# Orders in the second mixer and at the start of the second feed-forward: means joined inside a column, picks ahead of low halves, a root and a Silu table earlier

## What is computed

```python
def hybrid_mixer(h, ...):                       # h = rms_norm(x, norm_mix_w)
    proj = h @ w_in                             # 512 pool, 256 q, 256 k, 512 v, 16 gate, 512 r
    pool_out = multiscale_pool(p, pool_w, pool_scale)
    log_g = log_sigmoid(g_low @ gk_w2 + gk_b) / 16
    o = gla_chunked(q, k, v, log_g)             # chunks of 64, causal inside and between
    gla_out = rms_norm(o, gla_norm_w) * silu(r)
    return concatenate([pool_out, gla_out]) @ w_out

def conv_ffn_2(h, w_up, conv_w, conv_b, w_down):
    u = h @ w_up                                # 2 x 2816 columns
    u = conv_b + conv_w[0]*u[t-2] + conv_w[1]*u[t-1] + conv_w[2]*u[t]
    return (silu(gate) * val) @ w_down
```

## Time and profile before

| | us |
|---|---|
| median of 3 runs | 849.12 (848.76 to 849.17) |
| the profiled execution's own time | 849.34 |
| its span in the trace | 847.3 |
| PE busy | 835.3 (99%) |
| DVE busy | 577.3 (68%) |
| ACT busy | 476.9 (56%) |
| POOL busy | 353.2 (42%) |

### The profile page before, as it was taken

How to read it: one execution, slowest core, us unless ns; L and a number is a source line. 1 busy time by engine, 2 the same in 40 slices (tenths; PEclk the granted TensorE clock), 3 DMA queues, 4 the chain that set the end, 5 groups by cost and what they waited for, 6 DMA issues and landing times.

```text
span 847.3 us, 14837 instructions
## 1 busy us (share of the span) xinstructions
PE 835.3 (99%) x5858; PEld 766.1 (90%) x5858; DVE 577.3 (68%) x1214; ACT 476.9 (56%) x793; POOL 353.2 (42%) x173
## 2 busy tenths in 40 slices
PE   9999999999999999999999999999999999999997
PEld 4578999998899999999999988999999888888886
DVE  4789879886467896767677879686448445444445
ACT  7353345443766655555555864555447666666665
POOL 0000000001751598888887300200000788888883
PEclk9999999999999999999999999999999999999999
DMA  9998556654275556555555546364535556566651
GB/s 350 367 384 272 202 208 214 206 168 140 73 253 182 175 182 194 178 193 176 184 189 176 162 150 197 101 194 127 179 100 174 174 177 198 183 195 191 198 178 73
DMA packets 44742, 161.37 MB, mean 190 GB/s; under 512 B 5105, under 2 KB 5377, under 8 KB 43522
## 3 DMA queue, kind: packets, MB, share of 16 engines
q1 hardware_dynamic: 44384, 159.38, 58.0%
q10 hardware_dynamic: 290, 1.05, 0.3%
HBM read 159.37 MB, written 1.05 MB: 189 GB/s over the span
## 4 chain that ended last, share of the span: by engine, by line
PE 87%; DVE 6%; ACT 3%; DMA 2%; issue 1%; POOL 1%; ACTq 0%; DVEq 0%; POOLq 0%
PE bank L667 13%; PE bank L672 13%; PE bank L670 12%; PE bank L1104 9%; PE bank L1110 5%; PE bank L1193 2%; PE bank L1195 2%; PE bank L1197 2%; PE bank L1143 2%; PE bank L1141 2%; PE bank L1145 2%; DVE wlo L526 2%; PE bank L1003 2%; PE bank L769 1%; PE bank L771 1%; PE bank L775 1%
## 5 line engine op out<-in xcount | busy, mean ns | idle before, releaser
L526 POOL TENSOR_TENSOR wlo<-raw,whi 128x1024 fp32r<-128x1024 f32 (+1 forms) x147 | 334.8, 2300 | 407.2 <-ACT whi L1375 407.0
L1375 ACT ACTIVATE whi<-raw 128x1024 fp32r<-128x1024 f32 (+1 forms) x253 | 258.6, 1026 | 66.7 <-PE bank L672 22.6
L1824 DVE SCALAR_TENSOR_TENSOR accs<-bank,vec,accs 128x189 f32<-128x189 f32 (+4 forms) x440 | 161.1, 433 | 71.2 <-ACT accs L1687 71.2
L526 DVE TENSOR_TENSOR wlo<-raw,whi 128x1024 fp32r<-128x1024 f32 x106 | 129.0, 1229 | 29.1 <-ACT whi L1375 28.4
L667 PE MATMUL bank<-h,whi 128*128 128x256 f32 x504 | 143.7, 286 | 0.0
L672 PE MATMUL bank<-h,whi 128*128 128x256 f32 x504 | 142.3, 283 | 0.0
L670 PE MATMUL bank<-h,wlo 128*128 128x256 f32 x496 | 140.5, 283 | 0.7 <-DVE wlo L526 0.7
L667 PEld LDWEIGHTS bank<-h,whi 128*128 128x128 f32 x504 | 96.6, 192 | 0.7 <-issue 0.3
L672 PEld LDWEIGHTS bank<-h,whi 128*128 128x128 f32 x504 | 96.7, 192 | 0.0
L670 PEld LDWEIGHTS bank<-h,wlo 128*128 128x128 f32 x496 | 95.1, 192 | 1.1 <-DVE wlo L526 1.0
L1104 PE MATMUL bank<-h,whi 128*128 128x512 f32 x352 | 88.4, 392 | 0.5 <-DVE gl L1821 0.4
(11 more groups left out here) (362 smaller groups left out, 1851.0 us busy)
## 6 DMA issues: line engine op xcount, KB each, us to landing
raw<-in_up SPq DMA_DIRECT2D x88, 512.0 KB, 3.5
raw<-in_w_in SPq DMA_DIRECT2D x45, 512.0 KB, 4.5
raw<-in_down SPq DMA_DIRECT2D x44, 512.0 KB, 3.5
ada_sc<-in_ada SPq DMA_DIRECT2D x8, 1024.0 KB, 19.9
ada_kT<-in_adaT SPq DMA_DIRECT2D x16, 512.0 KB, 4.7
raw<-in_w_out SPq DMA_DIRECT2D x16, 512.0 KB, 4.5
raw<-in_w_in_t SPq DMA_DIRECT2D x12, 512.0 KB, 4.5
ada_sc<-in_adaT SPq DMA_DIRECT2D x8, 512.0 KB, 7.7
```

The lines of the kernel that those rows point to most:

```text
L526: return e.tensor_tensor(wlo[:, j % HL, 0:k], raw[:, j % RAW, 0:k], whi[:, j % HL, 0:k].bitcast(F32), ALU.subtract)
L1375: e.activation(whi[:, j % HL, 0:(k1 - k0) * 128], raw[:, j % RAW, 0:(k1 - k0) * 128], ACT.Copy).then_inc(S.hi.up(j))
L1824: return e.scalar_tensor_tensor(out=out, in0=a, scalar=s, in1=b, op0=o1, op1=o2)
```

## The change

It moves instructions; it adds one activation (of one element a partition) that loads Silu's table. Nothing of the arithmetic changes.

1. `means("down")` moves from before column 7 to inside it, after its ninth matmul; column 0 moves ahead of the gate's small matmul, and `spread("rsd")` moves from inside column 7 to inside column 0. On ACT the high half of column 3's chunk (`splits(ch("w_in2", 0) + HL)`) moves ahead of Exp and Ln. On DVE column 0's low half moves from ahead of the mean's copy to behind the two reciprocals.
2. Columns 12 and 13 become `late`. On DVE the four picks of the first half of the tokens come ahead of the low halves of chunks 14 and 15 and ahead of column 12's scaling.
3. In the second feed-forward the root for `wo` comes ahead of one `splits`, and `spread("wo")` one k-tile later; Silu's table is loaded in pair 1 ahead of its second `splits`.

```diff
@@ lin_wide @@
-                    if beside and k == 2:
+                    if beside and k == 3:
@@ pe, second mixer @@
-            means("down", M["ssum"][:, 0, :], 4, S.sums, ("down", 7), (S.by_row, "rsd"))
             slot, free = lin_ring.take(("w_in2", 7), S.raw2, 7)
-            lin("w_in2", 7, banks[slot][:, 0:L], hm, free, lambda: spread("rsd", aux_bank("down")[:, L:2 * L]))
+            lin("w_in2", 7, banks[slot][:, 0:L], hm, free,
+                lambda: means("down", M["ssum"][:, 0, :], 4, S.sums, ("down", 7), (S.by_row, "rsd")))
+            slot, free = lin_ring.take(("w_in2", 0), S.raw2, 0)
+            lin("w_in2", 0, banks[slot][:, 0:L], hm, free, lambda: spread("rsd", aux_bank("down")[:, L:2 * L]))
             slot, free = lin_ring.take("gate_low", S.zb, "zb")
...
-            for n in range(4):
+            for n in range(1, 4):
...
             def readout(h):
                 slot, free = lin_ring.take(("w_in2", 12 + h), S.raw2, 12 + h)
-                lin("w_in2", 12 + h, banks[slot][:, 0:L], hm, free)
+                lin("w_in2", 12 + h, banks[slot][:, 0:L], hm, free, late=h < 2)
@@ act, feed-forward @@
+            def silu_next():
+
+                e.activation(cst[:, 2:3], cst[:, 1:2], ACT.Silu)
...
-                    splits(ch(up, i + NFF) + HL)
                     if f == 1 and i == 0:
                         w.wait_ge(S.total, "wo")
                         root("wo", aux_bank("wo")[:, 0:2])
+                    if f == 1 and i == 1:
+                        silu_next()
+                    splits(ch(up, i + NFF) + HL)
+                    if f == 1 and i == 0:
                         by_row("wo", M["rsd2"][:, :], aux_bank("wo")[:, 0:L])
@@ act, second mixer @@
             az, eG, enG, eD = M["az"], M["eG"], M["enG"], M["eD"]
+            splits(ch("w_in2", 0) + HL)
             w.wait_ge(S.zb, "abs")
...
-            for n in (0, 1):
-                splits(ch("w_in2", n) + HL)
+            splits(ch("w_in2", 1) + HL)
             w.wait_ge(S.logg, "sum")
@@ dve, second mixer @@
-            los(ch("w_in2", 5) + HL)
+            los(ch("w_in2", 5) + HL - 1)
             w.wait_ge(S.total, "down")
...
             inverse("rsd")
             inverse("rs1")
+            los(ch("w_in2", 5) + HL)
             w.wait_ge(S.by_row, "rsd")
...
-            los(ch("w_in2_t", 3) + HL)
...
             for s in range(2):
-                readout(s)
+                if s:
+                    readout(s)
...
                           # the four picks of this s
+                if s == 0:
+                    los(ch("w_in2_t", 3) + HL)
+                    readout(0)
             readout(2)
```

## The result

The changed kernel takes 850.97 us, the kernel before 849.20 us (medians of 22 runs each, taken by turns). The ratio is 1.0018, with a 95% interval of 1.0011 to 1.0025: 0.9 to 2.1 us slower. One of the 22 runs of the changed kernel took 902.39 us at a granted clock of 0.848; it is left out of the ratio, and without it the median is 850.93. The profiled execution of the changed kernel took 851.18, its span is 849.2.

The account below looks back on a forecast made before the run. PE, busy 99%, bounds the kernel, with DVE's chain second. 849.34 + 2.17 (DVE's delay reaching PE) - 1.1 (feed-forward) = 850.4, or 850.2 against the 849.12 median; own range 849.4 to 850.9, wide range 848.0 to 852.4.

Parts of the forecast that it names:

- Mean inside column 7: Column 7: the mean waits for chunk 7's low half, starts at 488.5 instead of 486.47; first scaling 3.1 us later.
- Column 3's high half ahead of Exp: ACT before Exp and Ln: takes back most of the 3.1 us, leaving DVE 0.87 us late.
- the order of column 0 costs PE nothing: Column 0 ahead of the gate's small matmul: no PE cost, as that matmul needs a bank free by 494.85.
- The picks' cover: Behind column 12's scaling: earlier picks leave DVE idle 1.5 us for ACT's high half, making it another 1.48 late.
- DVE sets PE at 543: Head norms' spread: reciprocals 2.35 us late on DVE, less 0.18 slack, make PE 2.17 us late.
- Where PE stands: Before the head norms: PE waits out most of its 2.17 us at the last pooled matmul and column 15.
- Part 3: Second feed-forward: PE's waits at the spread and ahead of pair 3 go, -1.1 us (bounds -0.8 and -1.2).
- all waits go: Rival, 12%: all six PE waits near the change go and DVE has room; 3.2 us less, 845.9.
- Both DVE terms: Mixer delays of 0.87 and 1.48 us on DVE; rival, 16%, that one is absent: 848.7 or about 848.5.
- Column 3's high half is ready: Rival, 10%: ACT doesn't have this half ready before Exp, DVE keeps its whole delay; 3.3 us slower, 852.4.
- Part 3 brings 1.19: Feed-forward rival, 10%: these edits bring nothing, since another wait takes its place; 851.3.
- The table load did fit: Feed-forward rival, 8%: Silu's table load doesn't fit ACT's idle, value column's copy 1.4 later, gain only 0.6; 850.7.

Follow-up runs that it names:

- part 2 alone: Kernel before with columns 12 and 13 late and picks ahead of two low halves and column 12's scaling; 850.55 us against 849.00, ratio 1.0019.
- late columns alone: Kernel before with columns 12 and 13 made late and nothing else; 850.74 us against 849.47, ratio 1.0012.
- the kernel with the mean ahead: Changed kernel with the mean moved back ahead of column 7, spread still in column 0; 849.98 us against 849.47 for the kernel before, ratio 1.0004.
- ACT's order alone: Kernel before with one edit, column 3's high half ahead of Exp and Ln on ACT; 848.05 us against 849.27, ratio 0.9981.

## Why the prediction was right

The forecast was 850.2, 1.1 over the median before, and slower through DVE's chain less what the feed-forward gives back. The medians say 1.77 more, the stretches that the change touches 1.99 - 1.19 = 0.80 more. The measured 850.97 lies inside the wide range (848.0 to 852.4) and just above the forecast's own (849.4 to 850.9). The way of it, DVE's chain and not PE's own waits, is what the runs show.

- *Mean inside column 7:* said at 488.5, measured at 488.57 on the clock of before. The wait at its first low-weight matmul was 1.34 (1.5 said), the one at column 0 0.27 (0.3 said). First scaling 493.75 said, 493.68 measured.
- *Column 3's high half ahead of Exp:* log gate 502.0 said, 501.93 measured; next low half behind the Exp 506.86 said, 506.82 measured. This edit was read as a part of the repair; the runs show it to be the best line of the diff (M -2.11 alone), which PE's two moves, at 3.84, more than spend. The prediction had said that the order of column 0 costs PE nothing; that holds for PE's own instructions there, but the spread inside column 0 is what DVE stands for.
- *The picks' cover:* 1.5 us of idle said, 1.43 measured. The DVE term was 1.48 said; 2.14 of DVE's delay at the low half behind it (527.22 - 525.08) less 0.83 at the Exp makes 1.31. The four picks in front of two lows took 1.32 (524.24 - 522.92), not 1.43: I had taken their busy time where their step counts.
- *DVE sets PE at 543:* 2.35 said for DVE, 2.13 measured; PE 2.17 said, 1.99 measured. The slack was 0.14 and not 0.18: where PE waits there, it starts 0.22 behind the reciprocals (546.64 - 546.42), and before it was 0.36. With 0.14 it fits part 2 alone too (DVE +1.31, PE +1.17). It is wrong as a picture of part 1, where PE's delay (0.80) is DVE's (0.81, 543.46 - 485.74 against 543.15 - 486.24): there column 12's low half and the pick tie PE to DVE before 543 does. The kernel with late columns alone shows this tie best.
- *Luck:* part 1 was 0.87 - 0.18 = 0.69 said and 0.80 measured, part 2 1.48 said and 1.17 measured. The two misses go opposite ways, so the sum is nearer than its terms.
- *Where PE stands:* said at the last pooled matmul and at column 15. Column 15 has 0.35. Most of it, 1.79, is earlier, at the last pairs, which wait for the picks of the second half of the tokens to free their banks:

```profile
530.41 0.95 PE L1244 MATMUL bank<-q,k 64*128 64x128 f32 x8 [1.79 <-DVE A L2365]
```

- *Part 3:* -1.1 said, -1.19 measured. The term was kept below its starts' sum (0.6 + 0.57) for no good reason.
- *The rivals:* "all waits go" needed DVE to have room; part 2 alone takes two of them away and M grows by 1.17. Both DVE terms are there. Column 3's high half is ready: ACT makes it in the two from 494.69 to 496.69, and Exp starts at 500.38 in that trace. Part 3 brings 1.19. The table load did fit: the next activation starts 0.01 behind the load's end (669.52 against 668.23 + 1.28), and the value column's copy at 670.62 comes 2.79 behind the gate column's (667.83), as before (668.09 - 665.29 = 2.80). The drain of 1.38 us that the Trainium skill (ScalarE: Activation LUTs, What ACT_TABLE_LOAD costs) counts on top doesn't show.

What stays open is the rest of the measured 1.77 between the medians. By M and F the change makes 0.80, by the lowest times 0.78; the ratio's interval begins at 0.9. Whether the change also moves the kernel's start, the runs don't show.

## What to carry to other kernels

Where one engine is busy 99% of the time, find the engine that comes second and follow its chain to the next place where the first waits for it: a wait taken from the first is won only if that chain gets shorter too. Before work is moved out of a place, look at what the next instruction of the same engine waits for: work that stands there may be covering a round trip to another engine. And put what another engine prepares ahead of its own long waits: one high half ahead of Exp and Ln was worth 2.1 us, while PE's two moves of the mean and the spread cost 3.8.

## What the runs showed that I had not expected

The execution profiled of the changed kernel lost 1.14 us before 486 us, where both kernels are alike. Below are its windows, and under them those of the kernel before. The columns are us, then PE, PEld (PE's loading of weights), DVE, ACT and POOL busy, then the granted clock, the DMA share and GB/s.

```profile
14.00:15.00 1.00, 1.00 (x14) 0.86 (x17) 0.04 (x1) 0.26 (x1) 0.00 (x0) 0.92 0.99 410
15.00:16.00 1.00, 1.00 (x12) 0.21 (x4) 0.13 (x1) 0.00 (x0) 0.00 (x0) 0.50 0.98 410
16.00:17.00 1.00, 1.00 (x8) 0.80 (x5) 0.00 (x0) 0.68 (x2) 0.00 (x0) 0.50 0.98 397
17.00:18.00 1.00, 1.00 (x5) 0.87 (x4) 0.65 (x2) 0.65 (x1) 0.00 (x0) 0.50 1.02 406
```

```profile
15.00:16.00 1.00, 1.00 (x20) 0.52 (x8) 0.18 (x1) 0.25 (x1) 0.00 (x0) 1.00 1.04 434
16.00:17.00 1.00, 1.00 (x7) 0.50 (x5) 0.69 (x2) 1.00 (x2) 0.00 (x0) 1.00 0.94 381
```

From 15 to 18 us PE ran at 0.50 of the clock, the lower of its two levels (1.2 GHz), after a wait of 0.87 for x's squares at 11.3; before, it stayed at 2.4 GHz and shows no wait there, only 0.28 at 13.6. Five of the fourteen profiled executions here show a mean of 0.83 over 10 to 20 us, and they begin chunk 7's low half at 486.9 to 487.7, the other nine at 485.6 to 486.2. The wait alone doesn't tell them apart: the kernel with the mean ahead waited 0.83 there and kept the clock, that with ACT's order alone waited 0.77 and lost it. The times of the kernel before scatter by as much: of its 22, 15 lie from 848.7 to 849.5 and 7 from 850.3 to 851.4. That this is the same cause is likely and not shown. An effect under 1 us is thus better read from a distance inside the trace than from medians.
